# Seven half-size products in place of eight for the gate and up projections of two feed-forward networks

## The reference

```python
def swiglu(h, w_gate, w_up, w_down):
    return (jax.nn.silu(h @ w_gate) * (h @ w_up)) @ w_down

x = x + swiglu(rmsnorm(x, norm_ffn[layer]), ffn_w_gate[layer], ffn_w_up[layer], ffn_w_down[layer])
```

## Time and profile before

| | |
|---|---|
| time, median of 3 runs | 3339.05 us (3336.49 to 3340.81) |
| span of the profiled execution | 3331.8 us |
| TensorE busy | 3209.7 us, 96% |
| VectorE busy | 1777.9 us, 53% |
| ScalarE busy | 1320.5 us, 40% |
| GpSimd busy | 1321.6 us, 40% |

### The profile page before, as it was taken

How to read it: one execution, slowest core, us unless ns; L and a number is a source line. 1 busy time by engine, 2 the same in 40 slices (tenths; PEclk the granted TensorE clock), 3 DMA queues, 4 the chain that set the end, 5 groups by cost and what they waited for, 6 DMA issues and landing times. The chain is left out here.

```text
span 3331.8 us, 48271 instructions
## 1 busy us (share of the span) xinstructions
PE 3209.7 (96%) x16492; PEld 2656.2 (80%) x16492; DVE 1777.9 (53%) x3737; ACT 1320.5 (40%) x2239; POOL 1321.6 (40%) x836
## 2 busy tenths in 40 slices
PE   7999999989999999999999998999999999999999
PEld 6877787789988888888888765578887874578887
DVE  6514324888858787877877467542211236632211
ACT  5234433246653333333333455332222436632222
POOL 2223342279972222222221323444444337644443
PEclk9999999999999999999999999999999989999999
DMA  5321242145579999999997421033333420033322
GB/s 125 84 73 33 77 116 73 57 137 206 206 281 351 320 327 320 329 316 332 316 323 271 118 57 35 9 95 96 94 91 95 125 65 1 14 95 94 95 87 83
DMA packets 453450, 501.83 MB, mean 151 GB/s; under 512 B 77360, under 2 KB 397808, under 8 KB 435392
## 3 DMA queue, kind: packets, MB, share of 16 engines
q1 hardware_dynamic: 429792, 363.05, 35.4%
q0 software_dynamic: 18432, 134.23, 10.9%
q10 hardware_dynamic: 5088, 2.75, 0.3%
HBM read 457.86 MB, written 38.80 MB: 149 GB/s over the span
## 5 line engine op out<-in xcount | busy, mean ns | idle before, releaser
L125 POOL TENSOR_TENSOR w_low<-w_ring,w_high 128x1024 fp32r<-128x1024 f32 (+2 forms) x316 | 747.1, 2368 | 1080.6 <-ACT w_high L120 1050.5
L136 PE MATMUL ps<-h_low,w_high 128*128 128x512 f32 (+1 forms) x2432 | 906.7, 373 | 34.4 <-PEq L631 18.4
L138 PE MATMUL ps<-h_high,w_low 128*128 128x512 f32 (+1 forms) x2432 | 898.1, 369 | 0.0
L137 PE MATMUL ps<-h_high,w_high 128*128 128x512 f32 (+1 forms) x2432 | 897.7, 369 | 0.0
L136 PEld LDWEIGHTS ps<-h_low,w_high 128*128 128x128 f32 x2432 | 461.4, 190 | 101.3 <-POOLq L620 17.0
L137 PEld LDWEIGHTS ps<-h_high,w_high 128*128 128x128 f32 x2432 | 461.6, 190 | 58.5 <-issue 1.0
L138 PEld LDWEIGHTS ps<-h_high,w_low 128*128 128x128 f32 x2432 | 460.9, 190 | 56.3
L120 ACT ACTIVATE w_high<-w_ring 128x1024 fp32r<-128x1024 f32 (+3 forms) x318 | 323.6, 1022 | 140.6 <-PE ps L138 121.2
L138 PE MATMUL ps<-v_high,top_at 128*128 128x512 f32 x768 | 300.4, 391 | 0.0
L137 PE MATMUL ps<-v_high,top 128*128 128x512 f32 x768 | 300.3, 391 | 0.0
L136 PE MATMUL ps<-v_low,top 128*128 128x512 f32 x768 | 299.1, 389 | 0.0
(11 more groups left out here) (548 smaller groups left out, 5375.0 us busy)
## 6 DMA issues: line engine op xcount, KB each, us to landing
w_ring<-in_peer_uv_dram SPq DMA_DIRECT2D x128, 512.0 KB
u_raw<-in_peer_uT_dram SPq DMA_DIRECT2D x78, 512.0 KB, 5.1
w_ring<-in_peer_uT_dram SPq DMA_DIRECT2D x50, 512.0 KB, 3.8
w_ring<-in_ffn_w_gate_dram SPq DMA_DIRECT2D x44, 512.0 KB, 3.7
w_ring<-in_ffn_w_up_dram SPq DMA_DIRECT2D x44, 512.0 KB, 3.6
w_ring<-in_w_in_dram SPq DMA_DIRECT2D x36, 512.0 KB, 3.8
w_ring<-in_ffn_w_down_dram SPq DMA_DIRECT2D x32, 448.0 KB, 3.3
peer_gates<-room SPq DMA_DIRECT2D x6, 2048.0 KB, 7.8
```

What stands on the lines that cost most here:

```text
L125: return eng.tensor_tensor(rounded(low), whole, high, ALU.subtract)
L136: nc.tensor.matmul(out, rounded(w_high), rounded(x_low), start=start, stop=False, **more)
L137: nc.tensor.matmul(out, rounded(w_high), rounded(x_high), start=False, stop=False, **more)
L138: return nc.tensor.matmul(out, rounded(w_low), rounded(x_high), start=False, stop=stop, **more)
```

## The change

For pairs 2 to 21 the 2x8 block of weight tiles of one pair is cut into four quarters: a11, a12 (gate, first and last four k tiles) and a21, a22 (up, likewise), each 128x512 in SBUF. x is cut in four as well: first or last four k tiles, first 256 tokens (early) or last 256 (late). Gate and up for both token halves are then 8 products of a quarter of the weights with a quarter of x, of four k tiles and 256 columns each. The change computes them from 7 products of sums of quarters, by Strassen's scheme in Winograd's form. In detail:

- Once per network ScalarE writes x times the gains in full (`raw_x`), VectorE makes four differences of its quarters, and ScalarE and VectorE split these in high and low halves (`combos` and, in part, `h`).
- For each pair VectorE makes four sums of weight quarters (`sums`: s3 = a11 - a21, s1 = a21 + a22, s2 = s1 - a11, s4 = a12 - s2), s1, s2 and s4 in place. ScalarE rounds and GpSimd makes low halves of seven operands of 128x512 (n = 0 to 6). TensorE makes seven products into half banks x, y, z, v, three of which go on adding to a bank that is copied out in between.
- Out of PSUM come four copies by ScalarE (`keep`) and four additions by VectorE (`add`). The gate and the up result lie in SBUF thereafter, so that the scaling and the multiplication read SBUF in place of PSUM.
- Pairs 0 and 1 are computed as before. All turns are written out, no loop is left. The down weights have `combos` for their halves in place of buffers of their own.

The diff, cut to its core:

```diff
+    def tensor(pe):
...
+        for i in range(FIRST, KF):
+            for n in range(N):
+                pe.wait_ge(low, nth(i, n) + 1)
+                if n == 0:
+                    if i < 2 * FIRST:
+                        pe.wait_ge(made, i - 1)
+                    else:
+                        pe.wait_ge(up_added, 2 * (i - 1 - FIRST))
...
+                if n == 4:
+                    pe.wait_ge(p1_read, i - FIRST + 1)
+                if n == 5:
+                    pe.wait_ge(p5_read, i - FIRST + 1)
+                if n == 6:
+                    pe.wait_ge(u2_read, i - FIRST + 1)
+                w_high, w_low = ring(nth(i, n))
+                x_high, x_low = of_x[n]
+                for k in range(HK):
+                    rows_k = slice(k * P, (k + 1) * P)
+                    mm = product(nc, half_bank(i, "xyvzxzx"[n]), w_high[:, rows_k], w_low[:, rows_k], x_high[:, k, :], x_low[:, k, :],
+                                 start=(k == 0 and n < 4), stop=(k == HK - 1), skip_group_check=True)
+                mm.then_inc(product_done, 1)
...
+    def gpsimd(pool):
...
+        for i in range(FIRST, KF):
+            for n in range(N):
+                pool.wait_ge(high, nth(i, n) + 1)
+                high_of, low_of = ring(nth(i, n))
+                low_half(nc.gpsimd, low_of, of_w(i, n), high_of).then_inc(low, 1)
+        split_ahead.low(pool, nc.gpsimd)
...
+    def scalar(act):
...
+        for k in range(KD):
+            nc.scalar.activation(raw_x[:, k, :], c.xT[:, k, :], ACT.Identity, scale=c.gains[:, k:k + 1]).then_inc(gained, 1)
+        late.root(act)
+        split_tile(2)
+        for at, of, n in ((T1_AT, t1, 1), (T2_AT, t2, 3), (T4_AT, t4, 4)):
+            act.wait_ge(combined, n)
+            split_combo(combo(at)[0], of)
+        swish(0)
+        split_tile(3)
+        finish(0)
...
+        for i in range(FIRST, KF):
+            act.wait_ge(dest_low, i - 1)
+            keep(i, 0, p1_read, gate[:, i % 2, early], "x")
+            split(i, 4)
+            finish(i - 1)
+            split(i, 5)
+            split(i, 6)
+            act.wait_ge(made, i)
+            keep(i, 3, p5_read, up[:, late_t], "z")
+            split(i + 1, 0)
+            keep(i, 4, u2_read, gate[:, i % 2, late_t], "x")
+            split(i + 1, 1)
...
+            split(i + 1, 2)
+            swish(i)
+            keep(i, 6, u3_read, up[:, early], "x")
+            split(i + 1, 3)
+        finish(KF - 1)
...
+    def vector(dve):
...
+        def sums(i, which):
...
+            if which == 3:
...
+                if i > FIRST:
+                    dve.wait_ge(low, nth(i - 1, 6) + 1)
+                v.tensor_tensor(s3[:, 0, :], a11, a21, ALU.subtract).then_inc(s_made, 1)
+            elif which == 1:
+                dve.wait_ge(s_made, done + 1)
+                v.tensor_tensor(a21, a21, a22, ALU.add).then_inc(s_made, 1)
+            elif which == 2:
+                dve.wait_ge(low, nth(i, 0) + 1)
+                dve.wait_ge(s_made, done + 2)
+                v.tensor_tensor(a11, a21, a11, ALU.subtract).then_inc(s_made, 1)
+            else:
+                dve.wait_ge(low, nth(i, 1) + 1)
+                dve.wait_ge(s_made, done + 3)
+                v.tensor_tensor(a12, a12, a11, ALU.subtract).then_inc(s_made, 1)
...
+        def scale(i):
+            dve.wait_ge(gate_added, 2 * (i - FIRST) + 2)
+            v.tensor_tensor(gate[:, i % 2, :], gate[:, i % 2, :], c.rstd[:, :], ALU.mult).then_inc(scaled, 1)
+
+        def make(i):
+            rescale(i)
+            dve.wait_ge(up_added, 2 * (i - FIRST) + 2)
+            dve.wait_ge(rescaled, i + 1)
+            v.tensor_tensor(gate[:, i % 2, :], gate[:, i % 2, :], up[:, :], ALU.mult).then_inc(made, 1)
+            finish(i)
...
+        for i in range(FIRST, KF):
+            dve.wait_ge(p1_read, i - FIRST + 1)
+            dve.wait_ge(product_done, nth(i, 1) + 1)
+            add(i, gate[:, i % 2, early], "y", gate_added)
+            sums(i + 1, 3)
+            sums(i + 1, 1)
+            sums(i + 1, 2)
+            dve.wait_ge(u2_read, i - FIRST + 1)
+            dve.wait_ge(product_done, nth(i, 5) + 1)
+            add(i, gate[:, i % 2, late_t], "z", gate_added)
+            scale(i)
+            sums(i + 1, 4)
+            dve.wait_ge(u3_read, i - FIRST + 1)
+            add(i, up[:, early], "v", up_added)
+            dve.wait_ge(p5_read, i - FIRST + 1)
+            add(i, up[:, late_t], "x", up_added)
+            make(i)
```

More of the change, by code:

```diff
@@ L548, in projection @@
     x_high, x_low = ctx.sem("x_high"), ctx.sem("x_low")
-    if per_turn > 2 and (behind is None or own_halves):
+    if per_turn > 2 and (behind is None or own_halves) and not isinstance(w, DownWeights):
         c.more_halves = c.halves(ctx, "w", [P, per_turn - 2, max(w.kt) * P])
@@ L822, in project_scaled, with project_add @@
     project(c, w, {"act": act, "dve": dve}, ahead=ahead, before=before, behind_tile=behind_tile, tail=(0, 8))
-def project_add(c, w, dest, rhs, whole=None, ahead=None, before={}, next_gain=None, plain=None, first=None, ctx=None, ready=None, first_bank=0):
+def project_add(c, w, dest, rhs, whole=None, ahead=None, before={}, next_gain=None, plain=None, first=None, ctx=None, ready=None, first_bank=0, squares=None):
     nc = c.nc
@@ L832, in project_add @@
     with c.stage() if ctx is None else nullcontext(ctx) as ctx:
-        feed = None if next_gain is None else Feed(c, ctx, next_gain, tiles, plain)
+        feed = None if next_gain is None else Feed(c, ctx, next_gain, tiles, plain, squares)
         def dve(eng, i, wait_tile, bank_free):
@@ new lines, with __init__, ring_slots, half_slots @@
+class GateUpWeights:
+    per_turn = 4
+    def __init__(self, w_gate, w_up):
+        self.views = [w.rearrange("(k p) n -> p k n", p=P) for w in (w_gate, w_up)]
+        self.base, self.split, self.split_at, self.can_split = None, 0, 0, 2
+    def ring_slots(self, b):
+        return (b,)
+    def half_slots(self, b):
+        return (b,)
+    def flat(self, c, b):
+        return [*(buf[:, b, :] for buf in c.w_halves), c.w_ring[:, b, :]]
+    def first_in(self, c, b):
+        return self.loaded(c, b // 2, b % 2)
+    def loaded(self, c, i, up):
+        b = 2 * (i % 2) + up
+        return c.w_in[b].sem, self.base[b] + 16 * (i // 2 + 1)
+    def load_tile(self, c, sp, i, up):
+        b = 2 * (i % 2) + up
+        sp.dma_start(c.w_ring[:, b, :].rearrange("p (k n) -> p k n", n=P), self.views[up][:, :, i * P:(i + 1) * P]).then_inc(c.w_in[b].sem, 16)
+    def load(self, c, sp, i, b):
+        self.load_tile(c, sp, b // 2, b % 2)
+    def count(self, c):
+        self.base = [c.w_in[b].n for b in range(self.per_turn)]
+        for b in range(self.per_turn):
+            c.w_in[b].n += 16 * (KF // 2)
+        return True
@@ L905, in ready, with slots_free @@
+    def slots_free(act):
+        act.wait_ge(product_done, nth(KF - 1, N - 1) + 1)
     def ready(pe, b, x):
-        pe.wait_ge(dest_low, 2 + x + 1)
-    return projection(c, ctx, w, {"act": act, "dve": dve}, ahead=ahead, before={"act": late.root, "dve": invert}, between={1: {}}, behind_tile={(0, 0): late.sum},
-                      after={"dve": lambda eng: eng.wait_ge(dest_low, 2 * w.turns + 2)}), ready
+        pe.wait_ge(dest_low, x + 1)
+    return Programs(sync, gpsimd, tensor, scalar, vector, slots_free, None), ready, s3
@@ L1180, in ffn_weights @@
 def ffn_weights(w_gate, w_up, w_down):
-    gate, up, down = (w.rearrange("(k p) n -> p k n", p=P) for w in (w_gate, w_up, w_down))
-    def pair(i, b):
-        return [(ALL, (gate, up)[b % 2][:, :, bass.ds(i * (2 * P) + b // 2 * P, P)])]
+    down = w_down.rearrange("(k p) n -> p k n", p=P)
     parts = [KD, KF // 3, KF // 3]
@@ L1198, in ffn @@
     with c.stage() as ctx:
+        a_at = c.nc.sbuf_base + -c.used % LINE
         a = c.halves(ctx, "a", [P, KF, T])
-        first, ready = project_swiglu(c, ctx, w_gate_up, a, w_down)
-        project_add(c, w_down, c.xT, a, ahead=ahead, next_gain=next_gain, plain=plain, first=first, ctx=ctx, ready=ready, first_bank=4)
+        c.names += 1
+        raw_x = c.nc.alloc_sbuf_tensor_at(f"gained_x_{c.names}", [P, KD, T], F32, offset=a_at + (KF - KD) * T * 4)
+        first, ready, squares = project_swiglu(c, ctx, w_gate_up, a, w_down, raw_x)
+        project_add(c, w_down, c.xT, a, ahead=ahead, next_gain=next_gain, plain=plain, first=first, ctx=ctx, ready=ready, squares=squares)
 def store_normed(c, gained, out):
```

195 lines of the change are left out of this document (165 added, 30 removed).

## The result

The changed kernel takes 3517.0 us (3515.0 to 3518.8), the one before beside it 3339.9: a ratio of 1.0532, interval 1.0517 to 1.0548, 177.1 us slower. The forecast was 3516 us, from 177 us more. The profiled execution of the changed kernel has a span of 3517.1 us.

A forecast was written before the change was run, and what follows sets the result against it. TensorE bound the stage before; afterwards VectorE's and GpSimd's chained turns would. 14.6 + 18 x 15.38 + 10.5 = 302 us against 217, with starts +177 for both networks: span 3331.8 to 3509, plus 7.2, 3516 us; range 3410 to 3570.

The forecast's parts named there:

- TensorE's own work: Pairs 2 to 21: 84 matmuls of 256 columns at 0.119 us, 10.0 us a pair against 10.86 before.
- The turns: VectorE instructions with both inputs in SBUF and GpSimd's low halves exclude one another: 7 x 1.15 + 8 x 0.55 = 12.45 us a pair.
- The walk: One new pair followed from ScalarE's last copy out of PSUM (keep 6) to the next pair's: 15.38 us, TensorE working 10.0.
- The bounds of 14.4 and 16.4: Time of one new pair in us with all low or all high ends of the step times; 3476 or 3556 us in all.
- +88.6 a network: Time added to each feed-forward network by the twenty new pairs and the start; +177 us for both.
- The ends: Start and end of the new pairs: 3.5 us lost at the start, 14.6 for the first pair, 10.5 before the down projection.
- start to the first keep 6: Stage start with TensorE waiting 3.5 us for the fourth tile, then 14.6 us for the first new pair.
- keep 6 to the down product: From pair 20's last copy out of PSUM to the down projection, behind GpSimd's first split part of its weights: 10.5 us.
- the 7.2 us between span and median: Median before lay 7.2 us above the profiled span; kept, it turned the forecast span of 3509 into 3516 us.
- Better packing: Rival: VectorE's and GpSimd's work falls into one another's gaps, a pair of 12.45 to 14 us, 3410 to 3470 us; 20%.
- The fallen clock: Rival: TensorE's clock stays low after waits of 2 to 3 us, 16.5 to 18.5 a pair, 3560 to 3640 us; 10%.
- The TensorE-bound rival: VectorE and GpSimd do not exclude one another; TensorE stays the bound, 10.0 to 10.5 a pair, 3312 to 3332 us; 4%.

The follow-up runs named there:

- the first experiment: Changed kernel with GpSimd's low halves of pairs 2 to 21 replaced by two zero fills that only write SBUF: 3326.9 us in one run.
- the order experiment: Changed kernel with a second buffer for s3, so s3 and s1 need not wait for low half 6, and s2 and s4 behind gate's scaling: 3451.2 us.

## Why the prediction was right

**TensorE's own work.** 0.119 us for a matmul of 256 columns, 10.0 a pair: the first experiment, where TensorE has no gap, has 835 in 100 us, 0.1198 each and 10.06 a pair. The trace of before gave this within 1%. By the forecast's reckoning that leaves 13 ns beside the columns (2 x 0.1198 - 0.2262) where it had 12. Both figures of 12 came from one line through the two widths, so they were one reading and not two.

**The turns.** Right, and shown: the sums took 1.60 to 1.67 us as the earlier trace rows had them, and 0.69 as soon as GpSimd did not read. The rule of the Trainium skill that the prediction weighed ("SBUF — State Buffer", section "Who interferes with whom") has a second half, that a GpSimd instruction which only writes SBUF does not contend. The trace agrees with both: 1.67 us beside the low halves, 0.69 beside the fills. A blocked instruction of 512 elements lost 0.9 to 1.0 us.

**The walk.** 15.38 us forecast, 15.09 measured. Step by step, measured from keep 6 to the end of each step: low half 3 and the second scaling 2.41 (2.43 forecast), multiplication 4.11 (4.13), rounding 4.78 (4.88), its low half 5.50 (5.73), low half 6 7.89 (8.10), s3 9.70 (9.85), s1 11.40 (11.55), s2 13.10 (13.25), addition 13.43 (13.70), scaling 14.16 (14.42), SiLU 14.82 (15.08). No step is off by more than 0.3 us. The mis-sized terms are ScalarE's rounding with VectorE's low half behind it (0.21 too long together) and the addition from PSUM (0.33 where the prediction took 0.45, since it begins under the end of the instruction ahead). TensorE's waits came ahead of products 3 and 5 as forecast, 2.72 us for some 3, and 1.39 for 1.8, and the low halves took up to 1.7 us (1.74 at 2425.16). The cause of the chain is confirmed by what breaks it: the order experiment took away the wait of s3 and s2's place, and the pair fell to 13.30.

The bounds of 14.4 and 16.4 were not worked out right. With the low ends that the prediction names (VectorE's turn 0.53, GpSimd's 1.15, the addition 0.42) the walk ends at about 15.1, and with the high ones (0.69, 1.28, 0.69, keep 6 0.38) at about 17.1. So the measured 15.09 is its low end, and the upper side was wider than said. The totals of 3476 and 3556 also took 40 such pairs where the sum has 36, and +88.6 a network should be +88.2; both are small.

**The ends.** Here two terms were off, in the same direction, and the shorter pair paid for them. From the first matmul of the gate and up products to the first of the down product the stage took 327.9 us where the terms give 328.1:

| term | forecast | measured |
|---|---|---|
| start to the first keep 6 | 40.8 | 43.3 |
| 18 pairs | 276.8 | 271.6 |
| keep 6 to the down product | 10.5 | 13.0 |

The end: the prediction began the down product behind its *first* early part. TensorE waits for both, since GpSimd raises the count for the two at once (line 620):

```profile
2543.05 4.87 POOL L125 TENSOR_TENSOR combos_low<-w_ring,combos_high 128x1024 fp32r<-128x1024 f32 x2
...
2548.02 0.80 PE L136 MATMUL ps<-a_low,combos_high 128*128 128x512 f32 x1 [3.13 <-POOLq L620]
```

That is one more low half of 1024, 2.4 us. In the version that waits for each part by itself (and leaves GpSimd less to do) this wait is 0.60 us. The start: TensorE waited 2.83 us for the fourth tile, 3.5 forecast, but the tile behind the wait ran at a granted clock of 0.57 for 4 us, by which 1.7 us are lost (4 x 0.43): from 2240.49 to the first matmul of 256 columns at 2247.59 it took 7.10 us for 5.43. From there to the end of keep 6 the first new pair took 15.8 us where 14.6 were forecast. In it GpSimd's low half 6 took 2.27 us beside VectorE's low half of the last combination of x (`h_low`), itself 2.31 us where one alone takes 1.22, and s3 waits for low half 6; that this is the whole of the 1.2 us is likely and not shown. The wait that came out shorter takes back some 0.4:

```profile
2240.49 0.80 PE L136 MATMUL ps<-h_low,w_high 128*128 128x512 f32 x1 [2.83 <-POOL w_low L125]
...
2240.00:2244.00 4.00, 3.50 (x9) 2.82 (x10) 3.34 (x3) 1.36 (x3) 3.37 (x3) 0.57 0.45 131
```

Inside the pairs TensorE's slack hides such a stretch, as forecast; at the start there is none. So the sum fitted to 0.2 us partly by luck; its terms fitted to 2.5 us and, for 18 pairs, 5 us. The step from 3509 to 3516 was luck as well: the 7.2 us between span and median did not stay (3517.1 and 3517.0 after). The profiled execution of before lay below its median, and 7.4 us of that showed ahead of the first network.

**The rivals.** Better packing did not come by itself: arbitration and latencies repeated the same order in every pair, and only another written order brought it (3451 us, inside the forecast's 3410 to 3470 for it). The fallen clock is real, 0.83 to 0.97 in five stretches of 50 us, and inside the pairs costs nothing that can be told from none (4 us between the medians); at the start of the first network it costs the 1.7 us above.

The TensorE-bound rival missed nothing in its size: without the blocking, and with GpSimd's steps 0.3 us shorter, the kernel took 3326.9, and the rival had 3312 to 3332. It missed its condition.

## What to carry to other kernels

Before work is moved from TensorE to VectorE and GpSimd, sort VectorE's instructions by where their inputs lie: those with both in SBUF and GpSimd's reads are added up as turns of one resource, the rest is not. The sum of turns is a floor and no forecast: 12.45, 10.8 and 9.6 us stood against 13.30, 11.45 and 11.0 measured, and in the last VectorE's own work with the time it stands blocked was the bound. Leave one input in PSUM wherever the value comes from there, and place what is left by walking one period from the engine that ends last to itself. A factor that is the same for all rows of a product may be applied behind it, where the engine is idle; in this kernel that turned a loss of 0.25% into a gain of 0.6%.

## What was not expected of the hardware

Busy time can hold blocked time: VectorE, 97% busy by the windows, spent 2.7 of 11.0 us in each pair standing in GpSimd's turns. Only the durations of single instructions, 1.67 for 0.69, tell it, and an added-up list of solo durations gave 10.0 to 10.4 us where 11.0 were measured. And who comes first matters by itself: the scaling of gate took 1.34 us in the order experiment and 0.74 in the one without sums, where it began 0.15 us ahead of the GpSimd instruction that would have blocked it. The row of the order experiment:

```profile
2410.86 1.34 DVE L1165 TENSOR_TENSOR gate<-gate,rstd 128x512 f32<-128x512 f32 x1
```
